# A residual block's paired halves: one of four sums of weight blocks is made in place by an accumulating DMA

## The reference

```python
def swiglu(x, w_gate, w_up, w_down):
    return (jax.nn.silu(x @ w_gate) * (x @ w_up)) @ w_down

f = swiglu(rmsnorm(h, ffn1_pre_g), ffn1_w_gate, ffn1_w_up, ffn1_w_down)    # 2048 -> 5632 -> 2048
h = h + 0.5 * rmsnorm(f, ffn1_post_g)
z = rmsnorm(h, mix_pre_g) @ w_in                                           # 2048 -> 5120
y = concatenate([rg_lru part, short convolution part]) @ w_out             # 2048 -> 2048
h = h + rmsnorm(y, mix_post_g)
f = swiglu(rmsnorm(h, ffn2_pre_g), ffn2_w_gate, ffn2_w_up, ffn2_w_down)
h = h + 0.5 * rmsnorm(f, ffn2_post_g)
```

## Time and profile before

| | |
|---|---|
| median of 3 runs | 1784.06 us (1783.88 to 1785.47) |
| profiled execution | 1784.02 us, span 1781.9 us, granted TensorE clock 0.999 |
| TensorE busy | 1760.5 us, 99% |
| DVE busy | 1270.5 us, 71% |
| ScalarE busy | 916.0 us, 51% |
| GpSimd busy | 71.6 us, 4% |
| chain that ended last | TensorE 92%, DVE 3%, GpSimd 2% |
| read from HBM | 346.10 MB, 197 GB/s over the span |

### The profile page before, as it was taken

The page is one execution under the profiler, slowest core; times in us unless marked ns, Lnnn a source line. Parts: engine busy times, 40 slices in busy tenths (PEclk is TensorE's granted clock), DMA queues, the critical chain, the costliest instruction groups (busy, mean ns, idle before and its releaser), DMA issues.

```text
span 1781.9 us, 21916 instructions
## 1 busy us (share of the span) xinstructions
PE 1760.5 (99%) x7886; PEld 1448.9 (81%) x7886; DVE 1270.5 (71%) x1232; ACT 916.0 (51%) x989; POOL 71.6 (4%) x51
## 2 busy tenths in 40 slices
PE   8999999999999999999999999999999999999998
PEld 6788888888888888788888878788888888788886
DVE  6888888888864444655686467888888897854444
ACT  6554545555554344556654457545455545544442
POOL 5000000000000000100000016000000000000000
PEclk9999999999999999999999999999999999999999
DMA  7565655655575556665565657555656566566554
GB/s 231 199 207 192 200 200 192 200 197 190 167 289 192 178 179 222 198 204 175 164 193 171 205 162 251 191 192 196 201 190 210 188 195 199 191 225 217 197 184 150
DMA packets 136241, 351.15 MB, mean 197 GB/s; under 512 B 8172, under 2 KB 10356, under 8 KB 135284
## 3 DMA queue, kind: packets, MB, share of 16 engines
q1 hardware_dynamic: 136148, 350.32, 60.1%
q10 hardware_dynamic: 32, 0.01, 0.0%
HBM read 346.10 MB, written 4.19 MB: 197 GB/s over the span
## 4 chain that ended last, share of the span: by engine, by line
PE 92%; DVE 3%; POOL 2%; ACT 1%; DMA 1%; issue 1%; DVEq 0%; SPq 0%; ACTq 0%
PE ps L1210 15%; PE ps L1212 15%; PE ps L1211 15%; PE ps L1312 15%; PE ps L1314 14%; PE ps L1313 14%; PE ps L1307 1%; POOL x L479 1%; DVE u_lo L932 1%; DMA u_raw<-in_ffn_w_up 1%; PE ps L1434 0%; PE ps L1246 0%; ACT w_hi L534 0%; PE ps L1446 0%; DVE tsum L947 0%
## 5 line engine op out<-in xcount | busy, mean ns | idle before, releaser
L826 DVE TENSOR_TENSOR w_lo<-raw,w_hi 128x1024 fp32r<-128x1024 f32 x316 | 393.7, 1250 | 348.0 <-ACT w_hi L534 344.4
L534 ACT CAST w_hi<-raw 128x1024 fp32r<-128x1024 f32 x320 | 334.9, 1053 | 392.2 <-PE ps L1212 336.0
L623 ACT CAST u_hi<-u_raw 128x2048 fp32r<-128x2048 f32 (+1 forms) x160 | 280.0, 1751 | 163.8 <-DMA u_raw<-in_ffn_w_gate 101.4
L932 DVE TENSOR_TENSOR u_lo<-u_raw,u_hi 128x2048 fp32r<-128x2048 f32 (+1 forms) x160 | 331.3, 2087 | 43.7 <-ACT u_hi L623 42.5
L1210 PE MATMUL ps<-w_hi,hT_hi 128*128 128x512 f32 x832 | 324.6, 390 | 1.2 <-DVE w_lo L826 1.2
L1212 PE MATMUL ps<-w_hi,hT_lo 128*128 128x512 f32 x832 | 323.8, 389 | 0.0
L1211 PE MATMUL ps<-w_lo,hT_hi 128*128 128x512 f32 x832 | 323.7, 389 | 0.0
L1312 PE MATMUL ps<-u_hi,xT_hi 128*128 128x512 f32 x720 | 286.5, 398 | 4.4 <-DVE u_lo L932 4.4
L1314 PE MATMUL ps<-u_hi,xT_lo 128*128 128x512 f32 x720 | 280.8, 390 | 0.0
L1313 PE MATMUL ps<-u_lo,xT_hi 128*128 128x512 f32 x720 | 280.7, 390 | 0.0
L631 ACT CAST t_hi<-tsum 128x1024 fp32r<-128x1024 f32 x120 | 122.2, 1051 | 192.8 <-PE ps L1314 149.6
(11 more groups left out here) (142 smaller groups left out, 1843.9 us busy)
## 6 DMA issues: line engine op xcount, KB each, us to landing
raw<-in_ffn_w_down SPq DMA_DIRECT2D x176, 512.0 KB, 4.4
u_raw<-in_ffn_w_gate SPq DMA_DIRECT2D x80, 1024.0 KB, 5.1
u_raw<-in_ffn_w_up SPq DMA_DIRECT2D x80, 1024.0 KB, 5.0
raw<-in_w_in SPq DMA_DIRECT2D x80, 512.0 KB, 4.0
raw<-in_w_out SPq DMA_DIRECT2D x32, 512.0 KB, 4.6
raw<-in_ffn_w_gate SPq DMA_DIRECT2D x16, 512.0 KB, 4.5
raw<-in_ffn_w_up SPq DMA_DIRECT2D x16, 512.0 KB, 4.7
resid<-in_x SPq DMA_DIRECT2D x8, 256.0 KB, 8.1
```

The costliest lines, as they stand in the source:

```text
L534: sc.copy(w_hi[:, s], raw[:, s]).then_inc(hi_ready, 1)
L623: sc.copy(unit(u_hi, p)[:, 0:n], unit(u_raw, p)[:, 0:n]).then_inc(unit_hi, 1)
L826: ve.tensor_tensor(w_lo[:, s], raw[:, s], w_hi[:, s].bitcast(f32), ALU.subtract).then_inc(lo_ready, 1)
L932: ve.tensor_tensor(unit(u_lo, p)[:, 0:n], unit(u_raw, p)[:, 0:n], unit(u_hi, p)[:, 0:n].bitcast(f32), ALU.subtract).then_inc(unit_lo, 1)
```

## The change

U1 is no longer made by DVE into tsum. A new list on GpSimd (half_pair_sums) waits for the load of each unit with sums and issues a DMA that adds block B11 onto block B12 inside u_raw, 128 x 512 float32, with a completion semaphore pair_sum for each of the three units. The cast to u_hi and DVE's sums of those units wait for pair_sum. u_hi and u_lo are then made of all four blocks, so that U1's halves are blocks B12 of u_hi and u_lo, and M5 uses them; DVE makes two instructions of sums in place of three, and the first cast and the first subtraction of the sums are of one block (U2) rather than two. M5 is no longer behind t_lo.

```diff
--- before.py
+++ after.py
@@ -95,7 +95,7 @@
     SEVEN = (2, 4, 6)
     NS = len(SEVEN)
     B21, B22, B11, B12 = range(4)
-    U1, U2, V4, V3 = range(4)
+    U2, V4, V3 = range(1, 4)
     M1, M6, M7, XB, M5, M4, M2, M3 = range(8)
     FORM, n_forms = {}, 0
     for p in range(GP):
@@ -281,6 +281,7 @@
         unit_raw = [sem(f"unit_raw{n}") for n in range(4)]
         unit_hi, unit_lo = sem("unit_hi"), sem("unit_lo")
         unit_used = sem("unit_used")
+        pair_sum = [sem(f"pair_sum{n}") for n in range(NS)]
         sums_done = sem("sums_done")
         t_hi_done, t_lo_done = sem("t_hi_done"), sem("t_lo_done")
         bank_done = sem("bank_done")
@@ -292,6 +293,8 @@
         x32_done = sem("x32_done")
         form_sum, form_hi, form_lo = sem("form_sum"), sem("form_hi"), sem("form_lo")
         resid_kept, resid_back = sem("resid_kept"), sem("resid_back")
+
+        TS = (slice(U2, U2 + 1), slice(V4, V3 + 1))
 
         def unit_count(f, q, p):
             return lin(q, GP, UNITS * f + p + 1)
@@ -503,8 +506,20 @@
                 pool.tensor_tensor(form("D1", 3, 6, 3), tile(3, 1, 0, 3), tile(3, 1, 1, 3), ALU.subtract
                                    ).then_inc(form_sum, 1)
 
+            def half_pair_sums(f, q):
+
+                for n, p in enumerate(SEVEN):
+                    pool.wait_ge(unit_raw[p % 4], 16 * (UNITS // 4 * f + 2 * q + p // 4 + 1))
+                    b = unit(u_raw, p)
+                    pool.dma_start(b[:, B12], b[:, B11], accum_op=ALU.add).then_inc(pair_sum[n], 16)
+
+            def pair_sums(f):
+                for q in range(HALVES):
+                    half_pair_sums(f, q)
+
             forms(0)
             pre(0)
+            pair_sums(0)
             post(0)
             pool.wait_ge(w_used, starts["in"])
             pool.memset(xpad[:, :, 0:pad], 0.0).then_inc(pads_set, 1)
@@ -514,6 +529,7 @@
             splits(2)
             forms(1)
             pre(2)
+            pair_sums(1)
             post(2)
 
 
@@ -619,16 +635,17 @@
                 act.wait_ge(unit_raw[p % 4], lin(q, 32, 16 * (UNITS // 4 * f + p // 4 + 1)))
                 if q[1] == 0 and p < 2:
                     act.wait_ge(w_used, Place(starts[f"up{f + 1}"]).count(2 * GP - 3 + 2 * p))
-                n = 3 if p in SEVEN else 4
-                sc.copy(unit(u_hi, p)[:, 0:n], unit(u_raw, p)[:, 0:n]).then_inc(unit_hi, 1)
+                if p in SEVEN:
+                    act.wait_ge(pair_sum[SEVEN.index(p)], lin(q, 16, 16 * (HALVES * f + 1)))
+                sc.copy(unit(u_hi, p), unit(u_raw, p)).then_inc(unit_hi, 1)
 
             def sums_hi(f, q, p):
                 n = SEVEN.index(p)
                 if q[1] or n:
                     act.wait_ge(unit_used, seven_used(f, q, n, 1))
                 for h in range(2):
-                    act.wait_ge(sums_done, lin(q, 3 * NS, 3 * (NS * HALVES * f + n) + 2 + h))
-                    sc.copy(t_hi[:, 2 * h:2 * h + 2], tsum[:, (q[1] * NS + n) % 2, 2 * h:2 * h + 2]).then_inc(t_hi_done, 1)
+                    act.wait_ge(sums_done, lin(q, 2 * NS, 2 * (NS * HALVES * f + n) + 1 + h))
+                    sc.copy(t_hi[:, TS[h]], tsum[:, (q[1] * NS + n) % 2, TS[h]]).then_inc(t_hi_done, 1)
 
             def m1_copy(f, q):
                 it, c = q
@@ -925,25 +942,22 @@
 
             def half_lo(f, q, p):
                 dve.wait_ge(unit_hi, unit_count(f, q, p))
-                n = 4
                 if p in SEVEN:
-                    n = 3
-                    dve.wait_ge(sums_done, lin(q, 3 * NS, 3 * (NS * HALVES * f + SEVEN.index(p) + 1)))
-                ve.tensor_tensor(unit(u_lo, p)[:, 0:n], unit(u_raw, p)[:, 0:n], unit(u_hi, p)[:, 0:n].bitcast(f32),
-                                 ALU.subtract).then_inc(unit_lo, 1)
+                    dve.wait_ge(sums_done, lin(q, 2 * NS, 2 * (NS * HALVES * f + SEVEN.index(p) + 1)))
+                ve.tensor_tensor(unit(u_lo, p), unit(u_raw, p), unit(u_hi, p).bitcast(f32), ALU.subtract
+                                 ).then_inc(unit_lo, 1)
 
             def half_sums(f, q, p):
 
                 n = SEVEN.index(p)
-                done = 3 * (NS * HALVES * f + n)
+                done = 2 * (NS * HALVES * f + n)
                 dve.wait_ge(unit_raw[p % 4], lin(q, 32, 16 * (UNITS // 4 * f + p // 4 + 1)))
+                dve.wait_ge(pair_sum[n], lin(q, 16, 16 * (HALVES * f + 1)))
                 if q[1] or n >= 2:
                     dve.wait_ge(unit_used, seven_used(f, q, n, 2))
                 b, u = unit(u_raw, p), tsum[:, (q[1] * NS + n) % 2]
-                ve.tensor_tensor(u[:, U1], b[:, B11], b[:, B12], ALU.add).then_inc(sums_done, 1)
-                dve.wait_ge(sums_done, lin(q, 3 * NS, done + 1))
-                ve.tensor_tensor(u[:, U2], u[:, U1], b[:, B22], ALU.subtract).then_inc(sums_done, 1)
-                dve.wait_ge(sums_done, lin(q, 3 * NS, done + 2))
+                ve.tensor_tensor(u[:, U2], b[:, B12], b[:, B22], ALU.subtract).then_inc(sums_done, 1)
+                dve.wait_ge(sums_done, lin(q, 2 * NS, done + 1))
                 ve.tensor_tensor(u[:, V4:V3 + 1], b[:, B21:B11 + 1:2], u[:, U2:U2 + 1].broadcast_to([P, 2, W]),
                                  ALU.subtract).then_inc(sums_done, 1)
 
@@ -952,8 +966,8 @@
                 u = (q[1] * NS + n) % 2
                 for h in range(2):
                     dve.wait_ge(t_hi_done, lin(q, 2 * NS, 2 * (NS * HALVES * f + n) + h + 1))
-                    ve.tensor_tensor(t_lo[:, u, 2 * h:2 * h + 2], tsum[:, u, 2 * h:2 * h + 2],
-                                     t_hi[:, 2 * h:2 * h + 2].bitcast(f32), ALU.subtract).then_inc(t_lo_done, 1)
+                    ve.tensor_tensor(t_lo[:, u, TS[h]], tsum[:, u, TS[h]], t_hi[:, TS[h]].bitcast(f32), ALU.subtract
+                                     ).then_inc(t_lo_done, 1)
 
             def bank_sums(f, q, js):
 
@@ -1371,8 +1385,8 @@
                         last.then_inc(bank_done, 1)
                     three(bank(M2), a12, *raw_of(B21), False, False)
                     three(bank(M3), form("S4"), *raw_of(B22), False, False)
+                    three(bank(M5), form("S1"), *raw_of(B12), False, False)
                     pe.wait_ge(t_lo_done, lin(q, 2 * NS, 2 * (NS * HALVES * f + n) + 1))
-                    three(bank(M5), form("S1"), *sum_of(U1), False, False)
                     last = three(bank(M6), form("S2"), *sum_of(U2), first, end)
                     if end:
                         last.then_inc(bank_done, 1)
```

## The result

| | before | after |
|---|---|---|
| median | 1784.19 us | 1959.38 us (1955.25 to 1961.81) |
| ratio | | 1.098, 95% interval 1.097 to 1.100 |
| span of the profiled execution | 1781.9 us | 1960.0 us |
| TensorE busy | 1760.5 us | 1806.7 us |
| mean granted TensorE clock | 0.999 | 0.961 |

What follows compares the result with a forecast made beforehand. TensorE, 99% busy, was taken to bound the kernel, with the chain to u3 having nothing to spare. 1784.0 us plus 20·5.0 − 19.4 = 80.6 us gave 1864.6 us; range 1808 to 1935 us.

Steps and rivals of the forecast that it cites:

- u0 done, load of u4, sums of u4, u_lo of u3: Chain in each half of weight units u0 to u7, as long as TensorE's u1 and u2: 10.2 us.
- X: Time from a unit's load landing until its new GpSimd DMA has landed; taken between 2.2 and 7.0 us.
- 20 X − 19.4: Microseconds added over all halves by u3 starting later, less the shorter chain of sums; 80.6 us forecast.
- the bound given was 7.0: u2 has four units of lead, so its DMA was called safe up to X = 7.0 us.
- X = 5.0: New DMA beside u5's load: 2.2 us, 0.93 for a second pass, 1.86 for alternating engines.
- The 8.1 us row: Crowded 256 KB loads of x at the start: +142.6 us, +162 with u2 late; that rival 1946 us, chance 0.11.
- The clock, given 2 in 100: Rival, chance 0.02: halves about 91% busy, half clock for a tenth of 840 us, 84 us more, 1949 us.
- Paid once a half: The wait delays u3 only, as u5's chain runs in parallel with that stall; 1864.6 us, chance 0.82.
- 1.7 us to spare at any X: ScalarE's copy out of a transpose, behind u6's cast: done at 7.6 + X, needed by TensorE at 9.3 + X.
- Off the path, as said: DVE loses 41.3 us of additions; columns moved between tiles cancel beside TensorE, covered by DVE's idle 29%.
- The kernel can hardly gain: TensorE is busy 99% of 1781.9 us and lost only 4.4 us before a weight block's first product.

Runs made afterwards that it cites:

- (1): Also e1: changed kernel with u_lo of units 3 and 5 moved before the sums of units 4 and 6 in DVE's list; 1865.86 us, ratio 1.047.
- (3): Changed kernel, DVE's list as it is, SyncE holding the load of unit 5 until unit 4's adding DMA has landed; 1892.74 us, ratio 1.062.
- run 7: Changed kernel with only unit 4's sum made by the DMA, those of units 2 and 6 in place by VectorE; 1965.5 us, one run.
- run 5: Changed kernel with GpSimd's 60 DMAs copying B11 onto B12 instead of adding, so U1 is left out; 1902.5 us, one run.
- Run 8: Changed kernel with 20 added matmuls of zeros before unit 3 in each half; 1926.56 us, ratio 1.081.
- 4: Changed kernel with both DVE's exchanged steps and the held load of unit 5; 1859.31 us, ratio 1.043.
- 6: Changed kernel with unit 4's sum made in place by VectorE, units 2 and 6 still by DMA; 1888.41 us, ratio 1.060.
- run 10: Changed kernel without the DMA: VectorE adds B11 onto B12 in place, with its two steps exchanged; 1776.13 us, ratio 0.9954.
- run 2: Kernel before the change, with only the exchange of u_lo and sums in VectorE's list; 1775.1 us, ratio 0.9951.

## Why the prediction was wrong

- **Which engine bounds, and which chain is critical: right.** "u0 done, load of u4, sums of u4, u_lo of u3" had nothing to spare; the idle time is at L1312, released by u_lo, and moves away when the list of DVE is changed (1), or shrinks when the DMA is shorter (3).
- **Where the missing 97.5 us are.** The span grew by 178.1 us and the forecast was 80.6. Of the difference, 46.2 us are TensorE's longer busy time, the clock, for which the sum had nothing; 31.6 us are X at unit 4, 6.6 us in the mean rather than 5.0; 19.7 us are delays that 20 X − 19.4 leaves out.
- **The sum 20 X − 19.4: right, with one term too small.** At the constant X of run 7 it is 4% short of the idle time. In the changed kernel, X at unit 4 is 6.6 in the mean, which gives 112 us of the 131.9. The sum took every load of unit 4 to land after 5.0 us. In nine halves, with unit 2's slow DMA beside it, this load lands after 5.7 to 7.8 us; over all 20 halves that is 16.5 us of lateness, and both together are 129 us. TensorE pays part of this before unit 3 and 9.5 us before unit 2, most of them in even halves, where X at unit 2 is 7.1 to 7.5 and the bound given was 7.0.
- **X = 5.0: the first step that failed.** The prediction took the engines to alternate between the load and the DMA and doubled two passes. In the runs, the sum takes 3.3 us alone (forecast for two passes alone: 3.1, near), 4.1 to 5.0 when it is issued 0.6 to 0.8 us before the load, and 7.1 to 8.0 when the load is issued up to 0.3 us after it. The price of the neighbour is 4.3 us, not 1.9: in run 7, where every DMA is of that kind, X is 7.6. That the median over all 60 DMAs is 4.5, near the 5.0, is luck. The rows of before gave the coincidence itself (landing at 411.0, next load at 411.38); what to charge for it they did not. The 8.1 us row, taken as an extreme, was the nearest one in kind: a DMA of 256 KB that lands in a crowd. By it the idle time would have been 143 us. The Trainium skill's fit in "DMA: Bandwidth & Descriptors", section "Anatomy of one DMA — SWDGE (gpsimd) path", gives 2.6 us for 256 KB by my estimate. The lone copy of run 5 is a little under it (2.2 to 2.3 us), the lone addition over it (3.3).
- **The clock, given 2 in 100 and nothing in the sum: the second step that failed.** It is 46 of the 178 us. The argument compared shares, 91% busy against 93% at full clock in 60 to 84 us. But the idle time in those 24 us is one gap of 1.57 us (before unit 3); in the changed kernel it is one of 4.7 to 7.8 us in each half, and there the clock falls every time. The busy share of a half doesn't tell the two apart: the stretch of 48 us shown in run 3 is 94.5% busy, more than the 93% of rows 11, and its clock falls. Run 8 shows that the idle time is the cause: fill most of it, and most of the clock comes back. The price that the prediction named, 84 us, was nearly twice what it cost.
- **Paid once a half: right as long as unit 3 pays.** Runs 1, 4 and 6 show that it is one debt: with unit 3's way around it, units 2, 4 and 5 and the copy of ScalarE each have less than X to spare. That X would be shorter at unit 6 than at unit 4 was foretold, and for the right reason: 3.3 against 7.5 us (medians), with no load beside it. The statement "1.7 us to spare at any X" was derived with the stall in it, and fell with the stall.
- **Off the path, as said:** 38 us less of DVE, with the columns moved between tiles (run 10).
- **Idle time of before: undersized.** "The kernel can hardly gain", from 4.4 us of waits; run 2 gained 9 us, as about half of the small delays counted as busy.

The best kernel of the study is the one before with the exchange in DVE's list, 1775.1 us, 0.5% under it; with the sum in place on DVE it is the same within noise.

## What to carry to other kernels

A wait in an in-order list is paid by whoever stands behind it: before an operation is given a longer latency, list what is queued behind its consumer, and put first what doesn't depend on it. Here a DMA triggered by the landing of a load started just when the next load did, because a load takes 5.0 us and TensorE frees the next buffer 5.4 us after the last: price it by its time beside that load, or hold the load. And a stall has two prices, the gap and the slower clock behind it: look for single gaps of several microseconds, as a high busy share of the whole stretch does not rule the second price out.

## What the runs showed of the hardware

- A DMA of 256 KB from SBUF to SBUF on GpSimd's queue lands 2.3 us after its issue as a copy and 3.3 us as an addition, both alone; issuing the addition takes 0.86 us of GpSimd, the copy 0.54 us (medians 869 and 546 ns). With a load of 1 MB from HBM issued up to 0.3 us after it, the copy takes 3.6 to 5.7 us and the addition 7.1 to 8.0 us, once 9.2.
- It slows the loads in turn: in the changed kernel, loads of 1 MB that overlap it land after 4.9 to 7.8 us, 6.1 in the median; the loads of the halves of before, after 5.0.
- TensorE's granted clock went to 0.50 at all 20 gaps of 4.7 to 7.8 us in the changed kernel and stayed there for some microseconds of full work. At shorter gaps it fell at some and not at others, and length alone does not sort them. Two stretches of e1, the first right behind a gap of 3.15 us, the second right behind one of 1.85 us (columns as in rows 2):

```profile
370.50:374.50 4.00, 4.00 (x20) 3.38 (x21) 3.86 (x4) 3.71 (x4) 0.00 (x0) 1.00 0.35 144
1590.86:1594.86 4.00, 4.00 (x11) 3.15 (x12) 3.88 (x3) 0.76 (x1) 0.87 (x1) 0.57 0.94 298
```
